# Issuing the loads of expert slots 4 and 5 at the router's logits in a two-layer mixture-of-experts step

## The chip, the cores and the metric

The kernel runs on one core of one Trainium2 chip. The metric is the device time of one launch in microseconds (us). The kernel before was run three times: 1242.37, 1247.24 and 1248.42 us, median 1247.24 us. One more execution was taken with the hardware profiler; its own time is 1243.17 us, and all rows shown here come from it.

## What is computed

One step of a two-layer encoder on 544 frames (512 prompt frames and 32 sample frames) of width 1024. Layer 0 has an attention mixer and a gated recurrence; layer 1 has a gated short convolution. After each mixer comes a mixture of 32 experts, which is the part that matters here:

```python
g_logits = (xt @ w_group) + b_group                 # 4 groups
e_logits = ((xt @ w_expert) + b_expert)             # 32 experts, 8 per group
# best group, then the best two experts in it, with gates
h = silu(xt @ w1[e]) * (xt @ w3[e]) * gate          # w1, w3: 1024 x 256 for each expert
out = sum over chosen experts of h @ w2[e]          # w2: 256 x 1024 for each expert
```

Every expert's weights are three matrices of 1 MB in fp32 (1024 KB each), so one layer's mixture reads 96 such matrices whatever the routing is.

## The kernel before, in words

**The mixture of a layer.** Each engine has its own program, and the programs meet at semaphores. After the output projection of the mixer, VectorE writes the normed frames `XF` (line 1256). SyncE (SP) stores them to a DRAM tensor `x_dram` (line 420). TensorE transposes them (line 624) into banks from which ScalarE and VectorE fill `XT`; TensorE then multiplies `XT` with the router weights `wr` (line 886). These are the logits, and the last of these matmuls raises `lg_mm` to 2l+1 in layer l. A second small set of transposes (line 891) raises it to 2l+2.

**The router.** `route` on VectorE (lines 1525 to 1597), a chain of some 40 short instructions with a few TensorE matmuls in it (lines 896 to 906), works out which frame goes to which expert. It ends with `gidx` (line 1583), the list of row numbers, and `yidx` (line 1607). GpSimd (POOL) waits for `gidx` and for `x_out` (line 578) and issues the first two gathers of rows (line 571), an indirect DMA from `x_dram` into `xr[0]` and `xr[1]`; each gather serves a pair of experts. Their landing is told by `xr_in[0]` and `xr_in[1]`.

**The experts.** For each of 16 pairs TensorE transposes the gathered rows (line 919), waits for `w13_in` of the slot (line 952), multiplies with w1 and w3 (`hidden`, line 925, which raises `h_mm`), and after the gate and a transpose (line 931) waits for `w2_in` and multiplies with w2 (`rows_out`, line 936, which raises `y_mm`). POOL scatters the results to DRAM (line 575) and issues the gather of the pair after next (lines 582 to 584) when the current one has been transposed.

**The ring of weight slots.** There are six slots of 24 KB a partition: `w13_s` (16 KB) and `w2_s` (8 KB), at 36 + 24 s KB. Experts 0 to 3 of a layer are loaded ahead of the mixture (in the main list of SP, lines 464 to 471 and 488 to 503). Slots 4 and 5 lie at 132 to 180 KB. There they overlap `XT` (132 to 149 KB), `XF` (152 to 172 KB) and, in layer 1, part of `g_lo` and of the output weights; so experts 4 and 5 can be loaded only when these have been used.

**The order of SP.** SP's program is a list written out by hand, and it does nothing out of order. In `mixture(l)` it issues the five stores of `XF` (line 420), waits for their landing (`x_out`, line 421), waits for the first two gathers (lines 422 and 423), and issues six loads for experts 4 and 5 (line 388 twice and line 391 once for each). For each expert e from 6 on it waits for `h_mm` of expert e-6 and issues the w1 and w3 loads (line 388), then waits for `y_mm` of expert e-6 and issues the w2 load (line 391). All of these loads go through SP's one queue (q1 in the profile); the gathers and scatters go through POOL's (q0).

Nothing else of SP's program stands between line 421 and line 430. The waits at the loop's head count experts: `sp.wait_ge(h_mm, l * NE + e - 5)` is reached when expert e-6 has been through `hidden`.

Of the kernel before, what the change touches and what calls it, by code (L numbers as in the profile page):

```python
# [58 lines left out]
def hmoe_step(nc, x_prompt, x_sample, cache_a_k, cache_a_v, state_hgrn, state_conv, norm_mix, norm_ffn,  # L59
# [13 lines left out]
    with ctx:  # L73
# [213 lines left out]
        PAIRS = NE // 2  # L287
# [38 lines left out]
        def _(sp):  # L326
# [59 lines left out]
            def w13_load(l, e, s, done):  # L386
                for part, w in enumerate((w1, w3)):
                    sp.dma_start(w13[s][:, part, :, :], w[l, bass.ds(e, 1)].rearrange("e (p k) f -> p (e k) f", p=P)).then_inc(done, 16)  # L388

            def w2_load(l, e, s, done):  # L390
                sp.dma_start(w2s[s][:], w2[l, bass.ds(e, 1)].rearrange("e (a p) n -> p (e a) n", p=P)).then_inc(done, 16)  # L391

            def expert_load(l, e, part):
                s = SLOTS[l][e % 6]
                if part == 0:
                    w13_load(l, e, s, w13_in[s])
                else:
                    w2_load(l, e, s, w2_in[s])

            def first_load(l, j):  # L400
                for part in range(2):
                    expert_load(l, j, part)
# [10 lines left out]
            def conv_load(m, s):  # L413
                for a in range(3):
                    sp.dma_start(wc[s][:, :, a, :], wcv[a, bass.ds(m, 1)].rearrange("m p k n -> p (m k) n")).then_inc(wc_in[s], 16)

            def mixture(l):
                for c in range(NC):
                    sp.wait_ge(xn_ok, NC * (2 * l + 1) + c + 1)
                    sp.dma_start(x_dram[l][c * P:c * P + ROWS[c], :], XF[0:ROWS[c], c, :]).then_inc(x_out, 16)  # L420
                sp.wait_ge(x_out, 16 * NC * (l + 1))
                sp.wait_ge(xr_in[0], 16 * (PAIRS // 2 * l + 1))
                sp.wait_ge(xr_in[1], 16 * (PAIRS // 2 * l + 1))
                for j in (4, 5):
                    first_load(l, j)
                for e in range(6, NE):
                    sp.wait_ge(h_mm, l * NE + e - 5)
                    expert_load(l, e, 0)
                    sp.wait_ge(y_mm, l * NE + e - 5)
                    expert_load(l, e, 1)  # L430
                if l == 0:
                    sp.wait_ge(g_mm, 2 * PAIRS)
                    sp.dma_start(gmix[:], norm_mix[1:2, :].partition_broadcast(P)).then_inc(gmix_in, 16)
                    for s in range(2):
                        sp.wait_ge(y_mm, 27 + s)
                        conv_load(s, s)
                sp.wait_ge(y_mm, NE * (l + 1))
                sp.wait_ge(cnt_ok, l + 1)
                for j in range(4):
                    sp.wait_ge(scat[j], 16 * (NE // 4) * (l + 1))  # L440

                most = sp.value_load(cnt_i[0:1, l:l + 1], min_val=0, max_val=T)
                with sp.If(most > CAP), sp.Fori(0, ROUNDS - 1) as r:
                    with sp.If(most > CAP * r + CAP):
                        with sp.Fori(0, NE) as e:
                            sp.wait_ge(ov[l]["free"], r * NE + e + 1)
                            w13_load(l, e, 3, ov[l]["w"])
                            w2_load(l, e, 3, ov[l]["w"])
                        sp.wait_ge(ov[l]["free"], r * NE + NE + 1)
                        sp.nop(nofuse=True)  # L450

                both = y_dram[l].rearrange("(r b) d -> r (b d)", b=2)
                for c in range(NC):
                    for i in range(2):
                        first = i * T + c * P
                        sp.dma_start(yab[c][0:ROWS[c], i, :], both[first:first + ROWS[c], :]).then_inc(rows_in[c], 16)
# [13 lines left out]
            for j in (2, 3):  # L470
                first_load(0, j)
            mixture(0)


# [27 lines left out]
            for j in (2, 3):  # L502
                first_load(1, j)
            mixture(1)
            for c in range(NC):
                sp.wait_ge(h_ok, 3 * NC + c + 1)
# [1245 lines left out]
```

## Time and profile before

| | |
|---|---|
| median of 3 runs | 1247.24 us (1242.37 to 1248.42) |
| the profiled execution, its own time | 1243.17 us |
| its span in the trace | 1241.4 us, 19628 instructions |
| TensorE matmul busy | 1004.0 us (81%) |
| VectorE, ScalarE, GpSimd busy | 434.9 (35%), 282.8 (23%), 181.0 (15%) us |
| moved by DMA | 282.68 MB, mean 228 GB/s |
| share of SP's queue q1 in 16 engines' span | 57.3% |
| mean granted TensorE clock | 0.896 |

The span is the time from the first to the last instruction of one execution, and 1.8 us of the execution's own time lie around it. In the page's slices the span is cut in 40 equal parts of 31.0 us; a digit is the busy share in tenths, and GB/s is what the DMA engines moved. The mixture of layer 0 lies between about 404 and 698 us, that of layer 1 between about 938 us and the end.

### The profile page before, as it was taken

How to read it: one execution, taken by the hardware profiler on the slowest of the kernel's cores; microseconds unless marked ns; L12 is line 12 of the kernel's file. 1: busy time of each engine (PE TensorE's matmuls, PEld its weight loads, DVE VectorE, ACT ScalarE, POOL GpSimd, SP SyncE). 2: the span in 40 equal slices, each digit the busy share in tenths (PEclk: the TensorE clock that was granted, in tenths of full speed). 3: DMA queues.
4: the chain of work that ended last, by engine and by line, in shares of the span. 5: the costliest groups of instructions: out<-in, count | busy, mean ns of one | idle time of the engine just before them, and what ended most of it. 6: DMA issues, size and time to landing. Idle time of an engine off the chain costs nothing.

```text
span 1241.4 us, 19628 instructions
## 1 busy us (share of the span) xinstructions
PE 1004.0 (81%) x8375; PEld 775.7 (62%) x8375; DVE 434.9 (35%) x935; ACT 282.8 (23%) x543; POOL 181.0 (15%) x146
## 2 busy tenths in 40 slices
PE   5989999678998499777887179999994897877771
PEld 4988999544698365444443179999993563443440
DVE  5333573447625511101100654655346111101104
ACT  4244322025612112111111322121211111111110
POOL 4244421002000022111111000000000121111110
PEclk9999999757999699889989579999996899998886
DMA  6322221401176199999997703324574899999976
GB/s 210 87 73 91 79 81 38 110 13 50 42 271 258 42 414 416 416 417 415 417 417 288 230 1 102 94 59 152 204 107 170 326 416 416 415 416 417 415 302 225
DMA packets 114854, 282.68 MB, mean 228 GB/s; under 512 B 22955, under 2 KB 70103, under 8 KB 98357
## 3 DMA queue, kind: packets, MB, share of 16 engines
q1 hardware_dynamic: 105044, 263.66, 57.3%
q0 software_dynamic: 9728, 17.85, 3.9%
q8 instruction: 61, 1.00, 0.4%
q14 instruction: 21, 0.16, 0.0%
HBM read 270.57 MB, written 27.02 MB: 240 GB/s over the span
## 4 chain that ended last, share of the span: by engine, by line
PE 54%; DMA 21%; SPq 10%; DVE 9%; ACT 2%; issue 2%; POOL 1%; DVEq 0%; POOLq 0%; ACTq 0%
DMA w<-in_w_dram 16%; PE banks L1004 12%; PE banks L925 9%; PE banks L649 8%; PE banks L867 8%; SPq L388 6%; PE banks L936 3%; PE banks L648 3%; SPq L391 3%; DMA wab<-in_w_in_ab_dram 2%; DVE XF L1256 2%; DMA yab<-y_rows 1%; DVE H L1673 1%; PE banks L624 1%; POOL wab_lo L563 1%
## 5 line engine op out<-in xcount | busy, mean ns | idle before, releaser
L925 PE MATMUL banks<-w,xgT 128*64 128x256 f32 x2048 | 260.8, 414 | 79.7 <-DMA w<-in_w_dram 78.9
L925 PEld LDWEIGHTS banks<-w,xgT 128*64 128x64 f32 x2048 | 162.1, 150 | 187.2 <-DMA w<-in_w_dram 84.1
L1622 DVE TENSOR_TENSOR hh<-banks,sg 128x128 f32<-128x128 f32 x64 | 18.6, 291 | 421.7 <-ACT sg L1192 381.9
L575 POOL DMA_INDIRECT y_rows<-ys,yidx x64 | 63.6, 994 | 396.0 <-ACT ys L1200 393.2
L936 PE MATMUL banks<-w,hT 128*64 128x512 f32 x512 | 116.9, 598 | 0.0
L1004 PE MATMUL banks<-xc_hi,wc_hi 128*128 128x272 f32 x384 | 111.7, 291 | 1.4 <-DVE xc_lo L1269 1.4
L1004 PE MATMUL banks<-xc_hi,wc_lo 128*128 128x272 f32 x384 | 112.2, 292 | 0.0
L1004 PE MATMUL banks<-xc_lo,wc_hi 128*128 128x272 f32 x384 | 111.5, 290 | 0.0
L571 POOL DMA_INDIRECT xr<-x_rows,gidx x32 | 33.5, 1045 | 431.9 <-DVE yidx L1607 414.9
L649 PE MATMUL banks<-wab_hi,xc_hi 128*128 128x256 f32 (+1 forms) x320 | 91.7, 287 | 0.7 <-POOL wab_lo L563 0.7
L649 PE MATMUL banks<-wab_hi,xp_lo 128*128 128x256 f32 (+1 forms) x320 | 90.7, 284 | 0.0
L649 PE MATMUL banks<-wab_lo,xc_hi 128*128 128x256 f32 (+1 forms) x320 | 88.4, 280 | 0.0
L1192 ACT ACTIVATE sg<-banks 128x128 f32<-128x128 f32 x64 | 17.8, 277 | 308.6 <-PE banks L925 305.2
L563 POOL TENSOR_TENSOR wab_lo<-wab,wab_hi 128x2048 fp32r<-128x2048 f32 x14 | 67.3, 4816 | 119.6 <-ACT wab_hi L1043 119.6
L1004 PEld LDWEIGHTS banks<-xc_hi,wc_hi 128*128 128x128 f32 x384 | 73.4, 191 | 1.5 <-issue 1.5
L1004 PEld LDWEIGHTS banks<-xc_lo,wc_hi 128*128 128x128 f32 x384 | 73.4, 191 | 0.0
L1004 PEld LDWEIGHTS banks<-xc_hi,wc_lo 128*128 128x128 f32 x384 | 73.3, 191 | 0.0
L936 PEld LDWEIGHTS banks<-w,hT 128*64 128x64 f32 x512 | 34.1, 136 | 58.5 <-issue 54.6
L648 PE MATMUL banks<-xc_hi,wab_hi 128*128 128x272 f32 x192 | 55.6, 289 | 7.1 <-POOL wab_lo L563 7.1
L1200 ACT ACTIVATE ys<-banks 128x512 f32<-128x512 f32 x64 | 38.2, 597 | 97.8 <-PE banks L936 97.8
L649 PEld LDWEIGHTS banks<-wab_hi,xc_hi 128*128 128x128 f32 (+1 forms) x320 | 56.0, 175 | 1.7 <-POOL wab_lo L563 1.0
L624 PE MATMUL banks<-ident,XN 128*128 128x128 f32 (+1 forms) x80 | 15.3, 361 | 50.5 <-DVE XN L1256 31.7
(282 smaller groups left out, 1788.0 us busy)
## 6 DMA issues: line engine op xcount, KB each, us to landing
w<-in_w_dram SPq DMA_DIRECT2D x192, 1024.0 KB
wab<-in_w_in_ab_dram SPq DMA_DIRECT2D x13, 1024.0 KB, 5.0
wc<-in_w_in_c_dram SPq DMA_DIRECT2D x24, 512.0 KB, 5.7
yab<-y_rows SPq DMA_DIRECT2D x16, 512.0 KB, 6.9
wo<-in_w_out_ab_dram SPq DMA_DIRECT2D x4, 1024.0 KB, 5.1
x_rows<-XF SPq DMA_DIRECT2D x8, 512.0 KB, 9.9
wo<-in_w_out_c_dram SPq DMA_DIRECT2D x4, 1024.0 KB, 5.7
H<-in_x_prompt_dram SPq DMA_DIRECT2D x4, 512.0 KB, 8.4
```

Of the source, the lines that this page charges most:

```text
L388: sp.dma_start(w13[s][:, part, :, :], w[l, bass.ds(e, 1)].rearrange("e (p k) f -> p (e k) f", p=P)).then_inc(done, 16)
L391: sp.dma_start(w2s[s][:], w2[l, bass.ds(e, 1)].rearrange("e (a p) n -> p (e a) n", p=P)).then_inc(done, 16)
L563: pool.tensor_tensor(wab_lo[n % 3][:], wab[n % 3][:], wab_hi[n % 3][:].bitcast(F32), ALU.subtract).then_inc(w_lo, 1)
L571: pool.indirect_dma_start(xr[i][:, :], None, x_dram[l][:, :], bass.IndirectOffsetOnAxis(ap=index.bitcast(U32), axis=0), bounds_check=T - 1 ...
L575: pool.indirect_dma_start(y_dram[l][:, :], bass.IndirectOffsetOnAxis(ap=index.bitcast(U32), axis=0), ys[i][:, :], None, bounds_check=4 * T ...
L648: return pe.matmul(out, w[:, k, cols], x[:, k, t], **flags)
L649: return pe.matmul(out, x[:, k, t], w[:, k, :], **flags)
L867: last = pe.matmul(bank[i % 4][0:ROWS[c], 0:OW], z(a, k)[:, c * P:c * P + ROWS[c]], w(b, k, s), start=k == 0 and j == 0, stop=k == KT - 1 ...
L925: last = pe.matmul(bank[hb][64 * f:64 * f + 64, 0:2 * P].rearrange("p (w j) -> p w j", w=2), xgT[i][:, k, 64 * ab:64 * ab + 64], w13[s][:, ...
L936: last = pe.matmul(bank[6 + ab][64 * n:64 * n + 64, :], hT[ab][:, 64 * f:64 * f + 64], w2s[s][:, f, n * 512:(n + 1) * 512], start=f == 0, ...
L1004: last = pe.matmul(bank[3 * half + a][:, 0:HALF], w[s][:, k, a, :], x[:, k, half * HALF:(half + 1) * HALF], start=k == 0 and j == 0, stop= ...
L1200: act.activation(ys[e % 4][:], bank[6 + ab][:, :], ACT.Copy).then_inc(ys_ok, 1)
```

## The change

SP no longer waits for the first two gathers of rows before it issues the loads of experts 4 and 5. In their place it waits for the logits matmuls of the layer. The wait for the stores of `XF` (`x_out`) stays. Both layers take the change, since both call `mixture`.

```diff
                 sp.wait_ge(x_out, 16 * NC * (l + 1))
-                sp.wait_ge(xr_in[0], 16 * (PAIRS // 2 * l + 1))
-                sp.wait_ge(xr_in[1], 16 * (PAIRS // 2 * l + 1))
+                sp.wait_ge(lg_mm, 2 * l + 1)
                 for j in (4, 5):
                     first_load(l, j)
                 for e in range(6, NE):
```

## Rows read from the trace of the kernel before

**Rows 1.** The page: GB/s that the DMA engines moved, in 40 slices.
```profile
GB/s 210 87 73 91 79 81 38 110 13 50 42 271 258 42 414 416 416 417 415 417 417 288 230 1 102 94 59 152 204 107 170 326 416 416 415 416 417 415 302 225
```

**Rows 2.** The page: the chain that ended last, by engine.
```profile
PE 54%; DMA 21%; SPq 10%; DVE 9%; ACT 2%; issue 2%; POOL 1%; DVEq 0%; POOLq 0%; ACTq 0%
```

**Rows 3.** Windows: stretch, length, busy us (count) of PE, PEld, DVE, ACT, POOL, PEclk, DMA share, GB/s.
```profile
400.00:404.00 4.00, 1.09 (x4) 0.72 (x4) 3.70 (x5) 1.77 (x4) 0.00 (x0) 0.54 1.03 422
...
406.00:427.00 21.00, 8.16 (x66) 5.68 (x64) 13.18 (x50) 2.96 (x6) 0.37 (x1) 0.74 0.00 0
427.00:432.00 5.00, 1.00 (x5) 1.00 (x6) 0.90 (x4) 0.00 (x0) 1.83 (x2) 0.50 0.47 123
433.00:446.40 13.40, 13.02 (x98) 7.64 (x98) 2.36 (x6) 3.03 (x6) 1.51 (x2) 0.95 0.96 376
436.00:672.00 236.00, 197.72 (x1370) 109.87 (x1366) 25.61 (x78) 35.48 (x76) 43.45 (x43) 0.93 1.01 409
945.00:963.00 18.00, 5.80 (x43) 3.49 (x39) 11.97 (x46) 2.09 (x4) 0.24 (x1) 0.69 0.00 0
963.00:968.00 5.00, 1.77 (x8) 1.57 (x8) 0.87 (x4) 0.60 (x2) 1.82 (x2) 0.50 0.37 103
969.00:982.00 13.00, 12.90 (x96) 7.82 (x98) 1.67 (x5) 2.29 (x6) 1.55 (x2) 0.95 0.97 385
973.00:1205.00 232.00, 191.79 (x1354) 108.66 (x1350) 25.34 (x77) 35.19 (x75) 43.46 (x43) 0.93 1.00 409
```

**Rows 4.** Waits of SP's queue: who waited for whom, us in total, times, longest.
```profile
SPq L423 <- DMA xr<-x_rows,gidx: 59.1, 2, 30.6
```

**Rows 5.** Timeline of SP, layer 0: start us, duration us, instruction.
```profile
432.52 0.81 SPq L388 DMA_DIRECT2D w<-in_w_dram  x2
...
437.84 1.32 SPq L388 DMA_DIRECT2D w<-in_w_dram  x2
444.45 0.38 SPq L391 DMA_DIRECT2D w<-in_w_dram  x1
444.88 0.94 SPq L388 DMA_DIRECT2D w<-in_w_dram  x2
```

**Rows 6.** Timeline of SP, layer 1.
```profile
968.43 0.83 SPq L388 DMA_DIRECT2D w<-in_w_dram  x2
...
973.40 0.82 SPq L388 DMA_DIRECT2D w<-in_w_dram  x2
980.01 0.38 SPq L391 DMA_DIRECT2D w<-in_w_dram  x1
```

**Rows 7.** Chain of waits, layer 0, longest pieces: start us, us, what.
```profile
408.13 4.09 PE banks L886 x31
...
426.63 4.32 DMA xr<-x_rows,gidx
446.13 6.91 PE banks L925 x64
...
457.91 6.91 PE banks L925 x64
```

**Rows 8.** Chain of waits, layer 1, longest pieces.
```profile
942.32 6.12 PE banks L886 x31
...
962.76 3.42 DMA xr<-x_rows,gidx
```

**Rows 9.** Waits between 434 and 680 us.
```profile
PE banks L925 <- DMA w<-in_w_dram: 38.3, 12, 4.9
```

**Rows 10.** A window of 1 us in layer 1, columns as in rows 3.
```profile
970.00:971.00 1.00, 1.00 (x10) 0.71 (x8) 0.00 (x0) 0.00 (x0) 0.00 (x0) 0.83 0.80 295
```

**Rows 11.** All gathers (line 571), from DMA to landing, us.
```profile
DMA to landing us min/median/max: 3.4/8.6/10.0
```

**Rows 12.** Timeline of VectorE: the copies of XT in layer 0.
```profile
403.45 1.30 DVE L1261 COPY XT<-banks 128x512 f32<-128x512 f32 x2
405.36 0.69 DVE L1261 COPY XT<-banks 128x512 f32<-128x512 f32 x1 [0.61 <-PE banks L624]
```

## The prediction

> **What bounds the kernel now.** I read the slices of the page first. Ahead of the first mixture the DMA engines move 13 to 271 GB/s and between the two 1 to 230; in the slices 15 to 21 (434 to 652 us) and 33 to 38 (993 to 1179 us) they move 414 to 417 in every slice [rows 1]. The chain that ended last confirms it only in part: TensorE has 54% of it, but DMA has 21% and SP's queue another 10% [rows 2], so about a third of the chain is weight traffic. The windows give the rate of the two long stretches: 409 GB/s over 436 to 672 us and 409 over 973 to 1205 us, with a DMA share of 1.00 to 1.01 [rows 3]. In these stretches a pair of experts costs TensorE 11.8 us where it doesn't wait (457.91 - 446.13 [rows 7]), while its weights, six times 1.049 MB, take 6.29 / 0.409 = 15.4 us. The transfers are the slower side, TensorE waits 12 times for weights in layer 0, 38.3 us in all [rows 9], and sixteen pairs at 11.8 us are 189 us of the 236. So each mixture ends when its stream of weights ends.
>
> Just ahead of each stream stands a hole: 0 GB/s from 406 to 427 us and again from 945 to 963 us [rows 3], while the router picks experts and all six slots but two are full. SP stands at line 423 for 59.1 us in two waits, the longer 30.6 us [rows 4]; that is the wait the change removes.
>
> **The change, step by step.** *Moved earlier: six loads a layer.* The logits matmuls end at 408.13 + 4.09 = 412.2 us [rows 7] and at 942.32 + 6.12 = 948.4 us [rows 8]. The loads of expert 4 are issued at 432.52 [rows 5] and 968.43 us [rows 6]. They would go about 20 us earlier in each layer. The other wait ahead of them, for the stores of XF, must be over by then: nothing moves from 406 us and from 945 us on [rows 3]. From issue to flow I take 1.9 us: issue at 968.43, and 295 GB/s in the window 970 to 971, so that they set in at 970.3 [rows 6, 10]. So the 6.29 MB flow from 414.1 to 429.5 us, and from 950.3 to 965.7 us.
>
> *What can't move.* Expert 6 reuses the slot of expert 0. Its w1 and w3 are issued at 437.84 us [rows 5], as soon as expert 0 has been through `hidden`, and its w2 at 444.45 us, behind `y_mm` of expert 0; w1 and w3 of expert 7 follow at 444.88. In layer 1 the first two stand at 973.40 and 980.01 [rows 6]. These are TensorE's times, behind the first gather, and the change makes none of them earlier. The hole therefore doesn't close: it moves behind experts 4 and 5. The full 15.4 us a layer are not to be had.
>
> *What is gained.* I count bytes up to the moment from which the stream is full in both kernels, 446.4 us (444.45 + 1.9). The kernel before has by then moved 376 GB/s x 13.4 us = 5.04 MB since 433 us [rows 3]. The changed one has moved experts 4 and 5 (6.29 MB), the third gather (half of 123 GB/s x 5 us for two, 0.31 MB [rows 3]) and w1 and w3 of expert 6 (2.10 MB, 5.1 us from 439.7, with 1.6 us idle behind them): 8.70 MB. The lead is 3.66 MB, at 0.409 MB a us 8.9 us. In layer 1, up to 982.0 us: 6.29 + 0.26 + 2.10 = 8.65 MB against 385 x 13 = 5.01 MB [rows 3], again 8.9 us. From there on the queue always has work: TensorE frees a pair of slots every 11.8 us and the stream needs 15.4 for it. TensorE's slack of some 47 us in layer 0 (236 - 189) leaves room for the whole lead. Sum without a cost: 17.8 us.
>
> *The wait that is added.* SP now stands at `lg_mm`. Queued behind it on SP are only these loads; nobody waits for SP meanwhile. Cost nothing: the logits end 15 to 20 us before the old release.
>
> *What it can cost: the first gather.* It is on the path, 4.32 and 3.42 us from issue to landing in an empty fabric [rows 7, 8], and everything behind it, `h_mm` and so expert 6, slides with it. If the gather lands d later, the lead is 8.9 - d. The trace has no first gather beside weights, so I bound d. From below: 0, since the weights are over at 429.5 and the rows flow from 427 on; less than 0 is excluded, as its index comes from the router alone. From above: a gather in the full stream lands 8.6 us after its issue (median of 32 [rows 11]), 4.3 more than the first one. But that one meets a queue that never empties. Here the remainder is finite: 429.5 less some 428.0, where the rows begin to move, is 1.5 us in layer 0, and 965.7 less 964.0 is 1.7 us in layer 1. I take d = 1.6, the whole remainder ahead of the gather, since that is nearest to the case. Ends kept: 0 and 4.3.
>
> The Trainium skill (DMA: Bandwidth & Descriptors, Queues, rings and completion order) says that each engine goes round-robin between the queues that it has work for, a packet at a time, so that the gather shares instead of standing behind. By that rule d would be at most 1.2 us (the gather's own half of the 2.4 us of DMA time in 427 to 432 us), and the sum 15.4 instead of 14.6. The 8.6 us in the full stream are more than sharing alone would give, so the trace doesn't settle it.
>
> Sum: 2 x (8.9 - 1.6) = 14.6 us. The profiled execution took 1243.17 us, so it would take 1228.6. That execution lies 4.1 us under the median of 1247.24; against the median the forecast is **1232.6 us**.
>
> **The rivals.** *(a) The gather fares as in the full stream*, d = 4.3: 2 x (8.9 - 4.3) = 9.2 us, 1238.0 us. For it: all other gathers do. Against: the remainder of 1.5 us. *(b) No collision*, d = 0: 17.8 us, 1229.4 us. For it: the weights are nearly through. Against: the two overlap by my own count. *(c) Nothing comes of it*, the time stays at 1247: the lead is eaten, because the early loads don't start at the logits (the stores are late after all) or because the stream's end isn't what ends the mixture. Against: the silent window ahead and the DMA share of 1.0 up to 672 and 1205 us. *(d) Slower: the router's chain stretches.* Between logits and gather lie 426.63 - 412.2 = 14.4 us of some 40 short, dependent instructions, which now run beside a full load. If each took the factor that the gathers take in traffic (8.6 / 4.3 = 2), the gather would be issued 14.4 us later, the lead would be 8.9 - 14.4 = -5.5 us a layer, and the time 1247.2 + 11.0 = 1258.2 us. It decides the sign from a stretch of 62% on (8.9 / 14.4). Against: two copies of XT beside 422 GB/s [rows 3] take 1.30 us together, 0.65 each, and one at 405.36, where that traffic ends, 0.69 [rows 12].
>
> The Trainium skill (SBUF — State Buffer, SBUF: two separate sides) says that a DMA can't slow a compute instruction, having ports of its own; the copies agree, 0.65 beside 0.69 us.
>
> **How the numbers follow.** Forecast 0.50, (a) 0.22, (b) 0.16, (c) 0.08, (d) 0.04. Half a per cent is 6.2 us, about what a measurement can tell from no change; the forecast, (a) and (b) gain 9 to 18, so faster has 0.88, same 0.08, slower 0.04. The runs of before spread over 1242.4 to 1248.4. The low end is the lowest run less the 17.8 of (b), 1224.6, rounded to 1225; the high end takes in (a), 1238.0, and a little of the spread: 1240.
>
> **What would show it.** Right: SP's loads of experts 4 and 5 at about 412.5 and 948.7 us; over 400 GB/s from 414 to 429 us, then a new hole until about 440; the first gather landing 5 to 7 us after its issue; expert 6 issued near 439.5; the stretch of 409 GB/s ending some 7 us earlier in layer 0 and 14 to 15 in layer 1; VectorE's chain from line 1529 to 1583 unchanged at 13 us; the PE's wait for weights a little shorter. Wrong: a gather that lands over 8 us after its issue, a chain longer than 14 us, or a stream that starts earlier and ends where it ended.

## The result, and the profile after

The changed kernel takes 1232.08 us (median of 4 runs, 1231.30 to 1233.48) against 1246.76 us before (4 runs). The ratio is 0.9889 with a 95% interval of 0.9861 to 0.9917, a gain of 14.7 us between the medians; 14.6 were forecast, and 1232.6 us. The profiled execution took 1231.39 us (span 1229.7), 11.8 us less than the profiled one of before. (In the changed file SP's new wait is line 422 and all lines from 424 of the old file on are one lower: `hidden` is line 924, `rows_out` line 935.)

The page of the changed kernel, to be held against [rows 1] and [rows 2]:

```profile
GB/s 212 82 77 76 97 82 38 111 11 52 36 279 203 288 258 416 416 416 415 417 416 284 234 1 103 103 53 151 206 90 317 271 416 415 418 416 416 416 258 227
...
PE 56%; DMA 19%; DVE 9%; SPq 9%; ACT 2%; issue 2%; POOL 1%; another core or an unknown queue 0%; DVEq 0%; POOLq 0%; ACTq 0%
```

The slices are 31.0 us long before and 30.7 after, so they compare only roughly. The 14th (403 to 434 us before, 400 to 430 after) held 42 GB/s and now holds 288, but the 15th fell from 414 to 258. In layer 1 the 31st rose from 170 to 317 and the 32nd fell from 326 to 271. The hole was moved more than it was closed. The timeline of SP in layer 0 (start us, duration us, instruction), beside [rows 5]:

```profile
412.73 0.81 SPq L388 DMA_DIRECT2D w<-in_w_dram  x2
413.58 0.44 SPq L391 DMA_DIRECT2D w<-in_w_dram  x1
...
440.16 0.81 SPq L388 DMA_DIRECT2D w<-in_w_dram  x2
446.77 0.38 SPq L391 DMA_DIRECT2D w<-in_w_dram  x1
447.19 0.94 SPq L388 DMA_DIRECT2D w<-in_w_dram  x2
```

Experts 4 and 5 go 20 us earlier (432.52 to 412.73). Expert 6 goes no earlier, but 2.3 us later on the clock of the trace (437.84 to 440.16). The windows of the changed kernel (stretch, length, busy us and count of PE, PEld, DVE, ACT, POOL, PEclk, DMA share, GB/s), four stretches of layer 0 and three of layer 1:

```profile
416.00:429.00 13.00, 2.03 (x16) 1.46 (x16) 10.38 (x38) 0.21 (x1) 1.63 (x2) 0.57 1.01 419
...
438.00:441.00 3.00, 3.00 (x28) 2.12 (x26) 0.29 (x1) 0.28 (x1) 0.00 (x0) 0.94 0.00 0
...
446.00:449.00 3.00, 3.00 (x20) 1.22 (x18) 0.00 (x0) 1.10 (x2) 0.80 (x1) 1.00 0.48 150
449.00:655.00 206.00, 174.65 (x1228) 97.62 (x1226) 22.30 (x68) 30.88 (x67) 40.79 (x41) 0.93 1.02 415
...
944.00:959.00 15.00, 2.03 (x16) 1.46 (x16) 11.46 (x44) 0.42 (x2) 2.06 (x2) 0.60 1.00 414
...
966.00:968.00 2.00, 2.00 (x22) 1.45 (x20) 0.29 (x1) 0.28 (x1) 0.00 (x0) 1.00 0.00 0
...
974.00:976.00 2.00, 2.00 (x14) 0.86 (x12) 0.00 (x0) 0.88 (x2) 0.73 (x1) 1.00 0.45 92
```

That is the whole course: 419 GB/s while the router works, then little but the gathers until expert 6 may be loaded, a second gap at 446 to 449 us while SP stands at `y_mm` for one w2, and the full stream from 449 us on. Layer 1 repeats it.

The chain of waits of the changed kernel, its pieces at the head and at the tail of each stream (start us, us, what), and under it the tails of the kernel before, which were not shown:

```profile
408.55 4.09 PE banks L885 x31
...
427.06 4.64 DMA xr<-x_rows,gidx
...
434.62 8.96 PE banks L924 x64
...
641.43 24.23 DMA w<-in_w_dram
665.70 5.38 PE banks L924 x32
...
935.67 6.28 PE banks L885 x31
...
956.27 3.95 DMA xr<-x_rows,gidx
...
1167.97 24.18 DMA w<-in_w_dram
1192.19 5.63 PE banks L924 x32
```
```profile
647.70 24.23 DMA w<-in_w_dram
671.97 3.70 PE banks L925 x32
...
1182.68 22.84 DMA w<-in_w_dram
1205.56 3.70 PE banks L925 x32
```

From these I read the measure used below, **the length of a stream**: from the end of the logits matmuls (start and duration of their row added) to the landing of the last weights that TensorE waits for (likewise). Before: 671.9 - 412.2 = 259.7 us in layer 0 and 1205.5 - 948.4 = 257.1 in layer 1. After: 665.7 - 412.6 = 253.0 and 1192.15 - 941.95 = 250.2. So the streams gained 6.7 and 6.9 us. This measure is free of what comes ahead of the mixture, which varies: in some profiles below the logits of layer 0 end at 417 us instead of 412, with identical code ahead of them.

The prediction's account was in bytes moved up to a common point, and that can be checked directly. The windows of the first 45 us behind the logits, layer 0 and layer 1, and of the last 20 us of layer 1's stream, before and then after:

```profile
412.22:457.22 45.00, 28.22 (x209) 17.32 (x211) 17.22 (x62) 8.07 (x15) 6.26 (x6) 0.81 0.58 225
948.44:993.44 45.00, 29.20 (x213) 17.71 (x215) 17.20 (x62) 8.06 (x15) 6.39 (x7) 0.81 0.58 227
1185.52:1205.52 20.00, 15.18 (x98) 8.02 (x94) 1.72 (x6) 2.62 (x6) 1.96 (x2) 0.83 0.81 331
```
```profile
412.64:457.64 45.00, 27.89 (x201) 17.52 (x203) 17.10 (x62) 7.47 (x14) 6.28 (x6) 0.77 0.75 288
941.95:986.95 45.00, 28.68 (x211) 17.47 (x213) 17.19 (x62) 8.06 (x15) 6.12 (x6) 0.81 0.79 302
1172.15:1192.15 20.00, 14.40 (x112) 8.32 (x108) 1.96 (x6) 2.62 (x6) 2.96 (x3) 0.93 0.76 311
```

At the head 63 and 75 GB/s more over 45 us are 2.8 and 3.4 MB, which at 415 GB/s are a lead of 6.8 and 8.1 us. Layer 0 keeps 6.7 of it. Layer 1 keeps 6.9; of the difference 1.0 us is its tail, where the last 20 us moved 0.4 MB less than before.

### The profile page after: what moved, and what is told of

Its sections match the earlier page's. It is cut to its first block, busy times and chain, and to the rows that moved or that the text cites. A ratio compares the mean times of both kernels' runs of the same rounds, so it can differ in the third digit from the quotient of the medians.

```text
span 1229.7 us, 19628 instructions
## 1 busy us (share of the span) xinstructions
PE 1003.9 (82%) x8375; PEld 774.7 (63%) x8375; DVE 434.8 (35%) x935; ACT 282.9 (23%) x543; POOL 181.3 (15%) x146
## 4 chain that ended last, share of the span: by engine, by line
PE 56%; DMA 19%; DVE 9%; SPq 9%; ACT 2%; issue 2%; POOL 1%; another core or an unknown queue 0%; DVEq 0%; POOLq 0%; ACTq 0%
DMA w<-in_w_dram 14%; PE banks L1003 12%; PE banks L924 11%; PE banks L648 8%; PE banks L866 8%; SPq L388 6%; PE banks L935 4%; PE banks L647 3%; SPq L391 2%; DMA wab<-in_w_in_ab_dram 2%; DVE XF L1255 2%; DMA yab<-y_rows 1%; DVE H L1672 1%; PE banks L623 1%; PE banks L918 1%
## 5 line engine op out<-in xcount | busy, mean ns | idle before, releaser
L1191 ACT ACTIVATE sg<-banks 128x128 f32<-128x128 f32 x64 | 17.8, 278 | 297.8 <-PE banks L924 294.5
L648 PEld LDWEIGHTS banks<-wab_hi,xp_lo 128*128 128x128 f32 (+1 forms) x320 | 56.0, 175 | 0.4
```

Source lines behind the costliest of these rows:

```text
L648: return pe.matmul(out, x[:, k, t], w[:, k, :], **flags)
```

## The experiments

Twelve runs follow; e9 is the changed kernel once more and e11 the kernel of e8, so they are ten new kernels. Each ratio is to the kernel before on the same chip, with its 95% interval; medians of different chips differ by a few us, so ratios are compared, and lengths from the traces.

**One layer at a time.**

```diff
-                sp.wait_ge(lg_mm, 2 * l + 1)
+                if l == 0:
+                    sp.wait_ge(lg_mm, 2 * l + 1)
+                else:
+                    sp.wait_ge(xr_in[0], 16 * (PAIRS // 2 * l + 1))
+                    sp.wait_ge(xr_in[1], 16 * (PAIRS // 2 * l + 1))
```

> Edit: only layer 0 takes the new wait, layer 1 waits for the two gathers as before. My theory (each layer's stream gains its own lead of about 7 us): 1246.8 - 7.3 = 1239.5 us, with the whole gain between the logits of layer 0 and its last weights. Rival (the gain is made in layer 1 only, since what layer 0 gains is lost again in the convolution mixer behind it): 1246.8. Rival (all of it in layer 0): 1232.

Measured: 1237.8 us, ratio 0.9932 (0.9907 to 0.9956), 8.5 us by the ratio. Lengths: 252.5 us in layer 0, as the change, and 257.3 in layer 1, as before. Each layer has its own gain, and what layer 0 wins is not lost behind it.

**Releasing the loads later, across the gather.**

```diff
-                sp.wait_ge(lg_mm, 2 * l + 1)
+                sp.wait_ge(rk_mm, l + 1)
```

> Edit: SP waits for the rank matmuls (rk_mm) in place of the logits, some 8 us later; the loads of experts 4 and 5 then flow from about 423 to 438 us, right across the first gather. Theory A (the gather stands behind all weights already issued): it lands near 438, d = 9.8 us, and nothing is left of the lead, about 1247 us. Theory B (the gather fares as in the full stream, d = 4.3): lead 4.6 us a layer, 1237.6 us. Theory C (the queues share, d = 1.2): lead 7.7, 1231.4 us, hardly slower than the change. Rival on the gain itself (each us of earlier issue counts, one for one): 12 of the 20 us are left, 1238.

Measured: 1239.05 us, ratio 0.9944 (0.9922 to 0.9966). The chain of waits of this run, its two first gathers:

```profile
426.95 9.32 DMA xr<-x_rows,gidx
...
959.65 8.54 DMA xr<-x_rows,gidx
```

Against 4.32 and 3.42 us in the kernel before they land 5.0 and 5.1 us later: theory B, the full stream's 4.3, comes nearest. It isn't the 9.8 us of a gather that stands behind everything issued, nor the 1.2 us of even sharing. The lengths are 256.7 and 254.4, so of 6.7 and 6.9 us only 3.0 and 2.7 are left. In full, expert 6 is released 17.1 and 16.6 us after the gather's issue (444.06 - 426.95, 976.26 - 959.65) instead of 11.2 and 10.6, so d is 5.9 and 6.0, and my formula gives 8.9 - d = 3.0 and 2.9. The rival by earlier issue also said 1238 us, so this run doesn't part it from theory B; the next one does.

**Only one of the two experts early.**

```diff
                 sp.wait_ge(lg_mm, 2 * l + 1)
-                for j in (4, 5):
-                    first_load(l, j)
+                first_load(l, 4)
+                sp.wait_ge(xr_in[0], 16 * (PAIRS // 2 * l + 1))
+                sp.wait_ge(xr_in[1], 16 * (PAIRS // 2 * l + 1))
+                first_load(l, 5)
```

> Edit: expert 4 is loaded at the logits, expert 5 behind the two gathers as before. My theory (what counts is the bytes moved until expert 6 can be issued, and the full version leaves a hole there): 3.15 MB early are a lead of 7.7 us a layer, and no weights flow when the gather does, so no collision: 1246.8 - 15.4 = 1231.4 us, as fast as the change with half of it; the stream has no hole behind the gather. Rival (the gain goes with the bytes that start early): half of 14.7, 1239.4 us.

Measured: 1229.71 us, ratio 0.9860 (0.9830 to 0.9890). Half of the bytes bring the whole gain; the rival's 1239.4 is out. The windows of this run show why: an empty stretch up to the gather's issue at 426.8 us, and no hole from 435 us on.

```profile
422.00:427.00 5.00, 1.45 (x11) 1.01 (x11) 3.73 (x13) 0.00 (x0) 0.20 (x1) 0.50 0.00 2
...
435.00:655.00 220.00, 187.75 (x1325) 105.31 (x1322) 24.11 (x74) 33.41 (x72) 41.49 (x41) 0.93 1.02 415
```

The lengths are 252.3 (7.4 us gained, 7.7 expected) and 251.0 (6.1). In layer 1 the first 45 us moved 293 GB/s, a lead of 7.2 us, and the last 20 us 313 for the 331 of before, which costs 0.9: the same slow tail as in the changed kernel.

**The second gap: the order within a pair.**

```diff
-                for e in range(6, NE):
-                    sp.wait_ge(h_mm, l * NE + e - 5)
-                    expert_load(l, e, 0)
-                    sp.wait_ge(y_mm, l * NE + e - 5)
-                    expert_load(l, e, 1)
+                for e in range(6, NE, 2):
+                    for part, done in enumerate((h_mm, y_mm)):
+                        for i in range(2):
+                            sp.wait_ge(done, l * NE + e + i - 5)
+                            expert_load(l, e + i, part)
```

> Edit: the change, and in the loop from expert 6 on the loads of a pair go w1/w3 of e, w1/w3 of e+1, w2 of e, w2 of e+1, with their waits in that order. In the trace of the change the stream stands nearly still from 446 to 449 us and again near 975 us, because SP waits for y_mm of expert 0 while the slot of expert 1 is long free for w1/w3. My theory (holes ahead of the full stream are the lead): 1.9 us a layer back, 1232.1 - 3.8 = 1228.3 us. Rival (these holes cost nothing, since TensorE is behind there anyway and not the stream): 1232.1 us.

Measured: 1221.6 us, ratio 0.9795 (0.9765 to 0.9824). Both theories expected too little: it is 10.5 us under the change where mine gave 3.8 and the rival nothing. The timeline of SP and a window of this run:

```profile
444.19 4.26 SPq L388 DMA_DIRECT2D w<-in_w_dram  x4
450.80 2.10 SPq L391 DMA_DIRECT2D w<-in_w_dram  x2
```
```profile
448.00:455.00 7.00, 7.00 (x50) 3.68 (x50) 1.33 (x4) 1.79 (x3) 2.03 (x2) 1.00 0.99 420
```

The gap is gone, which is 1.9 us. The lengths, 248.9 and 245.3, are 4.1 and 4.9 us shorter than the change's. The other 2.2 and 3.0 us are near one w2 matrix (1.05 MB at 415 GB/s, 2.5 us), which suggested a cause: in the pair order w1/w3 of expert 31, the last weights that TensorE stands still for, are ahead of w2 of expert 30 instead of behind it. The runs that follow were to part the two.

**First pair only, last pair only, and the pair order without the change.** In e5 the new order is taken for the first pair alone, as here (the lines around it loop over the pairs and issue the loads in this order); e6 has `e == NE - 2` in the condition, e12 further down `e in (6, NE - 2)`; e7 is the kernel before with the loop of e4.

```diff
+                    if e == 6:
+                        order = ((e, 0), (e + 1, 0), (e, 1), (e + 1, 1))
+                    else:
+                        order = ((e, 0), (e, 1), (e + 1, 0), (e + 1, 1))
```

> Edit: the change, with the pair order of e4 for experts 6 and 7 alone, all other pairs in the old order. My theory of e4 (two separate gains): this one fills the hole behind expert 6's w1/w3, 1.9 us a layer, 1232.1 - 3.8 = 1228.3 us; the stream reaches its full rate by 447 us. Rival (e4's gain is all at the end of the stream): 1232.1 us.

> Edit: the change, with the pair order for experts 30 and 31 alone. My theory: w1/w3 of expert 31, which TensorE waits for last, stand one w2 (1.05 MB, 2.5 us) earlier in the queue, so 2.5 us a layer, 1232.1 - 5.0 = 1227.1 us, and the hole near 447 us stays. Rival (the end is set by the last w2 and not by w1/w3): 1232.1 us.

> Edit: the kernel before the change, with the pair order of e4 for all pairs. My theory: its stream has no hole near 447 us, as experts 4 and 5 are still flowing, so only the end gains: 1246.8 - 5.0 = 1241.8 us. Rival (the order is worth the 10.5 us of e4 by itself, with or without the early loads): 1236.3 us.

Measured: e5 1231.83 us, 0.9892 (0.9871 to 0.9914); e6 1225.21 us, 0.9839 (0.9819 to 0.9860); e7 1240.22 us, 0.9966 (0.9952 to 0.9980). The last pair alone is worth 6.2 us by the ratio (0.9889 - 0.9839, of 1246; e6's interval ends at 0.9860 and the change's begins at 0.9861), and without the early loads the pair order brings 4.2 us, with lengths of 258.0 and 255.0 (1.7 and 2.1 us shorter, 2.5 expected). The first pair alone shows nothing in the time; its lengths, 251.3 and 249.6, are 1.7 and 0.6 us shorter than the change's, inside what the medians of two chips can hide. Beside e9, the change's second profile below, they are 1.5 us shorter and 0.4 longer. The gap's 1.9 us are thus shown in the trace of one layer only.

In e6 TensorE no longer waits for the last weights in either layer, so the length can't be read. From the end of the logits to the end of the last w1/w3 matmuls (first and second row of each layer) it has 254.6 and 252.8 us:

```profile
410.45 6.45 PE banks L890 x31
...
664.52 6.93 PE banks L929 x64
...
937.14 5.94 PE banks L890 x31
...
1188.95 6.93 PE banks L929 x64
```

The change has 258.4 and 255.9 there, but e9 has 256.6 and 252.9. So the time and layer 0 speak for a gain at the end of the stream, and layer 1 shows it only against one of the two profiles of the change.

**Both ends.**

> Edit: the change, with the pair order for the first pair (6, 7) and the last (30, 31) only, the old order between. e4 (all pairs) stood at 0.9795 of before, the change at 0.9889, e6 (last pair) at 0.9839, e5 (first pair) at 0.9892. My theory (only the two ends count): as e4, 0.9795 to 0.980, and 249 and 245 us from the logits to the last weights that TensorE waits for. Rival (the pairs between count too, about 5 us of e4): as e6, 0.984.

Measured: 1220.98 us, ratio 0.9806 (0.9768 to 0.9843), as e4, and 248.6 us of length in layer 0 (in layer 1 TensorE no longer waits for the last weights, so the measure has no last wait there). The estimate favours the two ends; the interval doesn't exclude the rival's 0.984. Apart, the two ends gave 6.2 us and nothing, together 10.3 (0.9889 - 0.9806, of 1246); whether that is more than the noise of three ratios isn't shown.

**Earlier still, and away from the gather.** Slot 5 doesn't overlap `XT`, so expert 5 needs only the transposes of `XF`:

```diff
+                sp.wait_ge(xt_mm, NXT * (2 * l + 1) + 2 * NC)
+                first_load(l, 5)
                 sp.wait_ge(lg_mm, 2 * l + 1)
-                for j in (4, 5):
-                    first_load(l, j)
+                first_load(l, 4)
```

e10 has this edit alone, e8 and e11 have it with the pair order of e4. e9 is the unedited change beside them.

> Edit: e4, and expert 5 is loaded once TensorE has transposed XF (xt_mm), before the logits, expert 4 at the logits. The weights of both are then through some 4 us before the rows flow, so nothing collides. My theory (earlier is worth only the collision that it avoids, d of 0.3 to 0.5 us a layer in the change): 1221.6 - 0.8 = 1220.8 us. Rival (each us of earlier issue of half of the bytes counts): 4.5 us earlier a layer for half of the bytes, 1221.6 - 4.5 = 1217.1 us.

> Edit: none, the changed kernel once more, on the same chip as the next two, for a comparison in which front parts and chips don't differ. Expected 1232.1 us, and from the end of the logits to the end of the last w1/w3 matmuls 258.4 us in layer 0 and 255.9 in layer 1.

> Edit: the change, but expert 5 is loaded once TensorE has transposed XF, some 5 us before the logits end, and expert 4 at the logits. My theory (the lead is bounded by expert 6's release; being earlier removes only the collision with the gather, which delays that release by 1.9 us in layer 0 and 0.35 in layer 1): the layer's stretch from the logits to the last weights gets 1.9 and 0.35 us shorter, 1232.1 - 2.3 = 1229.8 us. Rival (each us of earlier issue counts): half of the bytes 5 us earlier, 2.5 us in each layer, layer 1 too, 1227.1 us.

> Edit: as e8, the fastest so far, on the same chip as e9 and e10. If the parts add up (collision 2.3, hole 1.7 and 0.6, last pair 2.5 a layer), it is 9.6 us under e9; the medians of different chips made it 15.3. Rival: the parts help each other, over 13 us.

By its median e8 lies at the rival's 1217.1 us and not at my 1220.8. But the kernel before is 3.0 us faster on its chip (1243.79), and by the ratio, 0.9790, it lies at my value (1220.8 of 1246.8 is 0.9791); the rival's 0.9762 is just outside the interval. e9 to e11 were made on one chip, so that their medians can be compared.

| run | us | ratio to before | length layer 0 | layer 1 |
|---|---|---|---|---|
| before | 1246.76 | 1 | 259.7 | 257.1 |
| change | 1232.08 | 0.9889 (0.9861 to 0.9917) | 253.0 | 250.2 |
| e9, change again | 1231.21 | 0.9894 (0.9865 to 0.9923) | 252.8 | 249.2 |
| e10, slot 5 first | 1228.95 | 0.9875 (0.9849 to 0.9901) | 251.5 | 248.8 |
| e8, with pair order | 1216.78 | 0.9790 (0.9766 to 0.9814) | 247.2 | 244.9 |
| e11, the same | 1220.22 | 0.9806 (0.9780 to 0.9832) | 247.0 | 244.3 |

e9 also says how far two executions of one kernel differ: its lengths are 0.2 and 1.0 us from the change's, and to the end of the last matmuls of line 924 it has 256.6 and 252.9 us where 258.4 and 255.9 were expected, since its last 32 matmuls took 3.70 us in both layers, for 5.38 and 5.63.

e10 is 2.3 us under e9, as expected, though the two ratios overlap. The lengths are 1.3 us shorter in layer 0 and 0.4 in layer 1. The rival's 2.5 in each must be corrected, since the wait for the stores stands ahead of the early load too: expert 5 is issued 4.4 us before expert 4 in layer 0 (410.12 and 414.56) and only 2.3 in layer 1 (937.59 and 939.84), which would be worth 2.2 and 1.1. What went with the gain is the release of expert 6, counted from the end of the logits: 27.5 us in e9 and 25.5 in e10 in layer 0, 25.5 and 25.3 in layer 1. So e10 leans to my theory, by less than its expectation promised; the run that settles it is e3. e11 is 11.0 us under e9, between "the parts add up" (9.6) and "they help each other" (over 13), nearer to the sum. Against e10, on the same chip, the pair order in the whole loop brings 8.7 us, and 4.5 and 4.4 us of length: of all the gains behind the change this is the best shown. The kernel of e8 and e11 beats both kernels: 26.2 and 24.2 us under before by the ratios.

## Why the prediction was right, and which terms were off

**What bounds the kernel** was read right. The stream's end moved with its head: 6.7 and 6.9 us at the tail of each layer, after 200 us at 415 GB/s. Only the third of the chain that was put down to weights [rows 2] is too much, since the 21% of DMA and the 10% of SP hold other transfers too; by line, the landings of `w` and the loads of lines 388 and 391 have 16.4, 6.4 and 2.8%, a quarter.

**What can't move** was the step that made the number. Had the gain been the 20 us of earlier issue, or the 15.4 us of the bytes, the kernel would have won 30 to 40 us. e3 (half the bytes, all of the gain) shows that the release of expert 6 bounds it, and e2 that the lead shrinks by as much as that release slides.

**The sum.** Forecast 7.3 us a layer at the stream; the profile has 6.7 and 6.9, e9 6.9 and 7.9. The formula was 8.9 - d, with d = 1.6 in both layers. What d stands for is the delay of expert 6's release behind the issue of the first gather: 437.84 - 426.63 = 11.2 us before [rows 5, 7] and 440.16 - 427.06 = 13.1 after, so d = 1.9 in layer 0; in layer 1 10.64 before (973.40 - 962.76 [rows 6, 8]) and 967.26 - 956.27 = 10.99 after, so 0.35. In layer 0 the size is right for half a wrong reason: the gather landed only 0.3 us later (4.64 for 4.32) and the rest came from TensorE, whose first `hidden` pair took 8.96 us for 7.40. In layer 1 the gather was 0.5 us later and `hidden` no longer. There the formula gives 8.5. The bytes at the head say 8.1 (8.2 in e9, with 303 GB/s), so the formula holds to 0.4 us, and the streams gained 6.9 and 7.9: in the change's profile 1.0 us was lost at the slow tail, in e9 (327 GB/s in the last 20 us) 0.2. Why the last 20 us run now at 331, now at 311 GB/s is open. Of the signs, the first gather was to land 5 to 7 us after its issue; it took 4.64 and 3.95, so the collision at the gather, for which the whole d was meant, was only 0.3 and 0.5 us.

**The clock at the tail** was missing from the sum. The last 32 matmuls of line 924 took 5.38 and 5.63 us after, 3.70 and 3.70 before: 1.7 and 1.9 us of each lead were given back in this execution. The granted clock was 0.66 from 1192 to 1198 us, and 1.00 in the same stretch before (1205 to 1210). In e9, the same kernel, they took 3.70 and 3.70, so it doesn't come with the change every time. Whether the change makes it likelier is open: of the 13 streams with early loads and the old order at their end (change, e1 to e3, e5, e9, e10) seven ended with more than 5 us, of the three without early loads none. Another 3.1 us came unforeseen in layer 0, where the last scatter landed in 3.45 us instead of 6.57 (in e9 it took 5.48, so it varies between executions of one kernel):

```profile
677.35 3.45 DMA y_rows<-ys,yidx
```
```profile
681.93 6.57 DMA y_rows<-ys,yidx
```

(after, then before). From the end of one layer's logits to the start of the convolution, line 1003 after and 1004 before, the profile gained 8.3 us, and from the logits of layer 1 to the end 5.2; between them it lost 1.4, and the stretch ahead 0.4. That is the 11.7 us between the spans, 2.9 less than the sum. The medians differ by 14.7, so the agreement to 0.1 us with the forecast is partly luck: the profiled execution of before lies 3.6 us under its median and that of the change 0.7. The interval of the gain is 10 to 17 us, which takes in 7.3 us a layer as well as 6 or 8.

**The page on queues.** The Trainium skill (DMA: Bandwidth & Descriptors, Queues, rings and completion order) has each engine go round-robin between its queues. e2 agrees that the gather isn't held until the weights are through (it would have been 9.8 us) and disagrees on the price: even sharing would give 1.2 us, the runs show 5.0 and 5.1.

**Rivals.** (a), d = 4.3, is real but needs the full overlap of e2. (b), d = 0, isn't far: the collision at the gather cost only 0.3 and 0.5 us, and in layer 1, where d was 0.35, (b) is nearer than the forecast's 1.6. By the time, its 17.8 us lie just outside the interval. (d), the router's chain, fell: from VectorE's first step behind the logits to the issue of the gather 426.63 - 412.32 = 14.3 us before and 427.06 - 412.74 = 14.3 after, with 419 GB/s beside it. (c) fell with the result.

## What to carry to other kernels

Where a stream of loads bounds a stage, a load released earlier is worth the bytes that are moved until the next load whose release can't move; work out that release first, since beyond it the same hole only reopens further on. Keep early loads clear of a gather that the path waits for: half of the bytes were as good as all of them (e3), and weights that flowed across the gather cost it 5 us (e2). And order the loads as they are consumed: the pair order brought 8.7 us on one chip (e11 beside e10), where half of the bytes earlier still had brought 2.3 (e10 beside e9). That most of it comes from the end of the stream, one matrix less ahead of the last awaited weights, is what e6 speaks for.

## What the runs showed of the hardware

**A late rise of TensorE's clock.** The windows of 434 to 438 us, after and before:

```profile
434.00:438.00 4.00, 3.62 (x18) 2.17 (x18) 0.52 (x1) 0.80 (x1) 0.99 (x1) 0.50 0.27 73
```
```profile
434.00:438.00 4.00, 4.00 (x36) 2.85 (x38) 0.00 (x0) 0.20 (x2) 0.73 (x1) 0.94 0.89 360
```

The granted clock is 0.50 of full speed (1.2 GHz) up to 434 us in both, after the router's stretch with little on TensorE. Before, it is at full speed (1.00, 2.4 GHz) from 435 us on; after, only from 439 on, although TensorE began its transposes just 0.75 us later (431.75 for 431.00). A first `hidden` pair of 8.8 to 9.0 us was seen in layer 0 in e1, e4, e5, e6, e9 and e12 too, which all load across the gather's start, and one of 7.4 to 7.6 in e3, e7, e8, e10 and e11, which don't (e2, with its late gather, has 8.3). In layer 1 this split isn't there: of those that load across, the change, e4, e9 and e12 have 7.4 to 7.7 and e5 and e6 8.7 and 8.8, and e10, which doesn't, has 8.1. So in layer 0 a start 0.75 us later went with 1.6 us more in the first pair; why the clock answers so is open.

**A clock that rose with the pair order.** With the pair order in the whole loop the mean granted clock was 0.903 to 0.917 in all twelve executions of e7 and 0.906 to 0.909 in the five of e8; the kernel before stood at 0.886 to 0.897 in every one. In all eight such streams (e4, e7, e8, e11) the last 32 matmuls took 3.70 us. So a part of e4's 10.5 us, up to the 1.7 and 1.9 us of the change's slow last matmuls, can be clock and not bytes; the lengths, which end ahead of these matmuls, don't contain it.

**An unexplained pause.** In the output projection of layer 1 VectorE stood 4.8 us for one bank where 2.4 are usual, with no releaser in the trace, while TensorE went on multiplying at a granted clock of 1.00. The same pause, 3.9 to 4.5 us long, is in the profiles of e1 to e4, e9 and e11, and not in the other seven, before among them:

```profile
910.26 4.73 another core or an unknown queue
```

It costs the changed kernel's profile some 2 us. It comes and goes between e8 and e11, which are the same kernel, so it isn't the change's.
